# Moving the expert search of tiles 0 and 1 in a decoder layer: a part per step in tile 3's attention, and tile 1's scores through the side banks

## What is computed

```
xn = rms_norm(h); proj = xn @ w_in                       # q, k, v of both mixers, indexer, gates
y_a = diff_attention(...) @ w_branch_a                   # 4 heads, two softmaxes each
y_b = dsa_attention(... top 128 keys by the indexer) @ w_branch_b   # 8 heads
h = h + (sigmoid(gate_a) * y_a + sigmoid(gate_b) * y_b) @ w_out
hn = rms_norm(h)
q = hn @ w_query                                         # 8 heads x 2 halves of 64
s = q . sub_keys                                         # 8 x 2 x 128 scores per token
s1, i1 = top_k(s[..., 0, :], 16); s2, i2 = top_k(s[..., 1, :], 16)
expert = 16 best of the pairs s1 + s2                    # per head, of 128 * 128 experts
g = softmax(best sums)
h = h + sum over picks of g * gelu(u[expert] . hn) * v[expert]
```

## Time and profile before

| | |
|---|---|
| median of 3 runs | 1787.48 us (1783.99 to 1790.81) |
| the profiled execution: its time, its span | 1786.4 us, 1784.5 us |
| TensorE (PE) busy | 1718.6 us, 96% of the span |
| VectorE (DVE) busy | 1333.6 us, 75% |
| ScalarE (ACT) busy | 702.6 us, 39% |
| POOL busy | 697.6 us, 39% |
| chain that ended last | PE 64%, DVE 16% of the span |

### The profile page before, as it was taken

How to read it: one execution, slowest core, us unless ns; L and a number is a source line. 1 busy time by engine, 2 the same in 40 slices (tenths; PEclk the granted TensorE clock), 3 DMA queues, 4 the chain that set the end, 5 groups by cost and what they waited for, 6 DMA issues and landing times.

```text
span 1784.5 us, 27405 instructions
## 1 busy us (share of the span) xinstructions
PE 1718.6 (96%) x10077; PEld 1538.3 (86%) x10077; DVE 1333.6 (75%) x3000; ACT 702.6 (39%) x1042; POOL 697.6 (39%) x478
## 2 busy tenths in 40 slices
PE   8999998989898999999999999999999999999998
PEld 6778776555655779999999999999999999999998
DVE  5475945647557779899999805974888888888886
ACT  5334235232323234366346535553333333333332
POOL 5244330000001235687777766786522222222220
PEclk9999998989998999999999999999999999999999
DMA  4122213525443645699989998998998889888882
GB/s 162 45 93 95 75 44 119 188 95 180 149 146 139 208 143 161 188 349 326 353 283 318 307 358 310 358 335 300 387 347 335 323 330 336 322 332 334 321 333 111
DMA packets 154183, 429.88 MB, mean 241 GB/s; under 512 B 15312, under 2 KB 49744, under 8 KB 149728
## 3 DMA queue, kind: packets, MB, share of 16 engines
q1 hardware_dynamic: 117040, 294.23, 47.3%
q0 software_dynamic: 36864, 134.23, 19.9%
q10 hardware_dynamic: 176, 0.07, 0.0%
HBM read 384.44 MB, written 44.04 MB: 240 GB/s over the span
## 4 chain that ended last, share of the span: by engine, by line
PE 64%; DVE 16%; ACT 2%; issue 2%; DMA 1%; DVEq 0%; ACTq 0%
PE psum L2055 30%; PE psum L1210 6%; PE psum L1280 6%; PE psum L1282 5%; PE psum L1281 5%; PE psum L1197 3%; PE psum L1309 2%; PE psum L1110 2%; DVE rows_sb L1726 2%; DVE hits L1759 2%; DVE hot L1840 2%; DVE hits L1756 2%; DVE pick L1760 1%; DVE hot L1837 1%; PE psum L1166 1%
## 5 line engine op out<-in xcount | busy, mean ns | idle before, releaser
L1538 POOL TENSOR_TENSOR ul<-u,uh 128x1024 fp32r<-128x1024 f32 x128 | 320.4, 2506 | 457.3 <-ACT uh L1448 455.8
L1280 PE MATMUL psum<-split,uh 128*128 128x384 f32 x1024 | 353.9, 346 | 1.1 <-POOL ul L1538 1.1
L2055 PE MATMUL psum<-wh,vl 128*128 128x384 f32 x1024 | 343.6, 336 | 0.0
L1282 PE MATMUL psum<-split,ul 128*128 128x384 f32 x1024 | 343.3, 335 | 0.0
L1281 PE MATMUL psum<-split,uh 128*128 128x384 f32 x1024 | 342.9, 335 | 0.0
L2028 POOL DMA_INDIRECT v_row<-in_v,tri x128 | 146.1, 1141 | 357.8 <-DVE mixed L2127 349.9
L1280 PEld LDWEIGHTS psum<-split,uh 128*128 128x128 f32 x1024 | 192.8, 188 | 3.1 <-issue 1.4
L1281 PEld LDWEIGHTS psum<-split,uh 128*128 128x128 f32 x1024 | 193.0, 188 | 1.4 <-issue 1.4
L1282 PEld LDWEIGHTS psum<-split,ul 128*128 128x128 f32 x1024 | 192.6, 188 | 0.0
L2055 PEld LDWEIGHTS psum<-wh,vl 128*128 128x128 f32 x1024 | 192.3, 188 | 0.0
L2055 PE MATMUL psum<-wl,vh_first 128*128 128x384 f32 x512 | 173.2, 338 | 0.0
(11 more groups left out here) (315 smaller groups left out, 3232.0 us busy)
## 6 DMA issues: line engine op xcount, KB each, us to landing
u<-in_u SPq DMA_DIRECT2D x128, 512.0 KB
v<-in_v SPq DMA_DIRECT2D x64, 1024.0 KB
act_mat<-act_w SPq DMA_DIRECT2D x128, 192.0 KB
w<-act_mat SPq DMA_DIRECT2D x64, 384.0 KB
wraw<-in_w_wide SPq DMA_DIRECT2D x18, 1024.0 KB, 5.0
gate<-gate_mat SPq DMA_DIRECT2D x128, 128.0 KB
w_low<-in_w_branch_b SPq DMA_DIRECT2D x8, 1024.0 KB, 5.1
w_high<-in_w_branch_a SPq DMA_DIRECT2D x8, 1024.0 KB, 5.3
```

The costliest lines, as they stand in the source:

```text
L1280: nc.tensor.matmul(out, high[:, c], dense_x[0][:, c], start=(c == 0), stop=False)
L1282: last = nc.tensor.matmul(out, low[:, c], dense_x[0][:, c], start=False, stop=(c == DC - 1))
L1538: nc.gpsimd.tensor_tensor(ul[:, n % U_COLS], u[:, n % U_COLS], uh[:, n % UH_COLS].bitcast(F32), ALU.subtract).then_inc(s["u_low"], 1)
L2055: mm = nc.tensor.matmul(bank(m, c)[:, 0:WIDTH], lhs, rhs, start=first and k == 0 and p == 0, stop=final and p == 2)
```

## The change

Tile 0's search parts get other steps: finding at 36 to 40 instead of 36, 37, 40, 41, 43; pairing and the first two parts of the best at 41; picking out at 43, 44, 45, 46 instead of 49, 49, 50, 51; settling at 47 instead of 52. Tile 1's scores are no longer multiplied in one go at step 50 but in two products on the side banks at steps 45 and 46, as tile 0's are at 33 and 34, and ScalarE copies them one step later each; its search begins at step 48 instead of 52 and is settled at 58 instead of 63. TensorE's step 47 now waits for those copies before it uses the side banks. The picks of tile 0 are turned one pair of columns sooner (`AHEAD[1]` 14 instead of 15), and with them every later start, turn and the gathers.

```diff
-SCORE_FIRST, SCORE_FIRST_REST, SCORE_SECOND = 33, 34, NT * UNITS + 2
-FIND_AT = ((36, 37, 40, 41, 43), (52, 53, 54, 55, 56))
-PAIR_AT = (44, 57)
-BEST_AT = ((44, 47, 48, 48, 48), (58, 58, 59, 59, 60))
-PICK_AT = ((49, 49, 50, 51), (61, 61, 62, 62))
-SETTLE_AT = (52, 63)
+SCORE_FIRST, SCORE_SECOND = (33, 45), (34, 46)
+FIND_AT = ((36, 37, 38, 39, 40), (48, 49, 50, 51, 52))
+PAIR_AT = (41, 53)
+BEST_AT = ((41, 41, 42, 42, 43), (53, 54, 54, 54, 55))
+PICK_AT = ((43, 44, 45, 46), (55, 55, 56, 57))
+SETTLE_AT = (47, 58)
...
-AHEAD = (0, 15, 9, 9)
+AHEAD = (0, 14, 9, 9)
...
                     elif j == TURN_HN:
-                        if t == 1:
-                            pe.wait_ge(s["s_out"], 2)
+                        if 1 <= t <= 2:
+                            pe.wait_ge(s["s_out"], 2 * t)
...
-                if step == SCORE_FIRST:
-                    pe.wait_ge(s["keys_loaded"], 16)
-                    pe.wait_ge(s["streamed"], 4)
-                    route(0, 0, SIDE)
-                if step == SCORE_FIRST_REST:
-                    pe.wait_ge(s["s_out"], 1)
-                    route(0, 1, SIDE)
-                if step == SCORE_SECOND:
-                    pe.wait_ge(s["scores_used"], len(PLAN))
-                    pe.wait_ge(s["pT_ready"], len(ALL_UNITS))
-                    route_halves(1, 0, 2)
+                for r in range(2):
+                    if step == SCORE_FIRST[r]:
+                        pe.wait_ge(s["keys_loaded"], 16)
+                        pe.wait_ge(s["streamed"], 2 * (r + 2))
+                        route(r, 0, SIDE)
+                    if step == SCORE_SECOND[r]:
+                        pe.wait_ge(s["s_out"], 2 * r + 1)
+                        route(r, 1, SIDE)
                 if step >= FIRST_COLUMN:
                     column(step - FIRST_COLUMN)
-            pe.wait_ge(s["s_out"], 4)
+            pe.wait_ge(s["scores_used"], len(PLAN))
             route_halves(2, 2, SIDE)
...
-                if step == SCORE_FIRST + 1:
-                    score_out(0, 0, SIDE)
-                if step == SCORE_FIRST_REST + 1:
-                    score_out(0, 1, SIDE)
+                for r in range(2):
+                    if step == SCORE_FIRST[r] + 1:
+                        score_out(r, 0, SIDE)
+                    if step == SCORE_SECOND[r] + 1:
+                        score_out(r, 1, SIDE)
...
-                if step == BEST_AT[0][-1] + 1:
-                    exps(0)
+                for r in range(2):
+                    if step == BEST_AT[r][-1] + 1:
+                        exps(r)
...
-                if step == SCORE_SECOND + 1:
-                    score_out(1, 0, 0)
-                    score_out(1, 1, 2)
                 if step > FIRST_COLUMN:
                     column(step - 1 - FIRST_COLUMN)
-                if step == BEST_AT[1][-1] + 1:
-                    exps(1)
```

More of the change, by code:

```diff
@@ L876 @@
 FIRST_PAIR = TAIL_COLUMNS // 2
-assert TAIL_COLUMNS % 2 == 0 and FIRST_PAIR + 7 < TURNS_AT[1]
+assert TAIL_COLUMNS % 2 == 0 and FIRST_PAIR + 6 < TURNS_AT[1]
 assert TAIL_AT < PAIRS and AHEAD[2] > STORES and AHEAD[3] > STORES
```

## The result

The changed kernel takes 1801.11 us in the median of four runs (1799.08 to 1803.69), the kernel before 1785.93 us beside it (1783.99 to 1790.81): ratio 1.0077, with a 95% interval of 1.0051 to 1.0103. That is 15.2 us slower, where +4.5 was forecast, and above the end of the range. The profiled execution took 1799.37 us, span 1797.6 us.

The account below looks back on a forecast made before the run. TensorE was taken to bound the kernel, over 90% busy in nearly all slices. The terms 6.4 - 2.1 + 0.2 gave +4.5 us, 1790.9 on the profiled execution and 1792.0 for the median; range 1785 to 1798.

Parts of the forecast that it names:

- The late chain of steps 44 to 48: VectorE's added picking out and settling make TensorE wait for the normed and scaled rows, 6.4 us in all; chance 0.62.
- the clock term: Query product behind the two pauses in steps 47 and 48: low clock costs 0 to 1.2 us more, taken as 0.
- the prediction's list of signs: What the profile should show, including waits of 3 us and more for step 47's row and about the same before the query product.
- the sentence on the clock: The skill's "activity releases the throttle": by it alone the query product would run wholly at the low level, some 6 us more.
- The old product, -2.1: Step 50: tile 1's old scores product goes away, saving 2.06 us, with 3.45 us as the other end.
- Steps 51 to 62: Between attention and last search: tile 1's search called done long before; its new place got no cost.
- The first turn, +0.2: Turn of tile 0's picks, two columns sooner: slack of 6.9 us becomes 0.1 us late, taken as 0.2; gathers cost 0.
- The second turn: Next turn of picks among the columns, called tile 2's: it keeps its distance, so its wait of 1.82 us stays.
- Filled gaps: Rival: tile 1's products on the side banks keep the clock full around steps 45 to 48, -5.5 us, 1782.0; chance 0.09.
- Late picks: Rival: POOL's conversions hold the last search's VectorE passes, tile 0's picks 4.3 us late, +10.0 us, 1797.5; chance 0.15.
- Hidden: Rival: VectorE's new parts fit between the products and the clock stays, about 0, 1787; chance 0.14.

Follow-up runs that it names:

- e3: The changed kernel with tile 0's last part of picking out at step 48 instead of 46 and its settling at 49 instead of 47: 1794.18 us, ratio 1.0043.
- f1: The kernel before with only tile 1's scores through the side banks at steps 45 and 46, search and AHEAD as before: 1786.15 us, ratio 1.0005.
- e1: The changed kernel with tile 1 settled at step 60 instead of 58, behind tile 3's normed row: 1795.68 us, ratio 1.0048.
- h3: The kernel before with AHEAD[1] 14 instead of 15 and nothing else: 1789.24 us, ratio 1.0019.
- h2: The kernel of f3 run once more for a second profile: 1790.23 us in one run.
- e2: The changed kernel with AHEAD[1] back at 15: 1801.44 us, ratio 1.0076.
- f3: The kernel of e4 with AHEAD[1] 14 again instead of 15: 1790.83 us, ratio 1.0034.
- e4: The changed kernel with tile 0's last picking out at step 48, settling at 49 and 60, and AHEAD[1] 15: 1784.91 us, ratio 0.9995.
- p1: The kernel before, unchanged, run again for a second profile: 1789.73 us in one run.
- f2: The kernel before with only tile 0's search at the new early steps, tile 1 and AHEAD as before: 1795.17 us, ratio 1.0049.

## Why the prediction was wrong, step by step

**The late chain of steps 44 to 48: right.** The normed row was forecast at 552.65 us and came at 549.04; in this execution step 42 was 2.9 us earlier, so 0.7 us of a difference is left. From step 42 on, the transposes came 36.55 us later where it had been 32.55, +4.0 against +4.6; the query product +5.2 against +6.4; the transposes of tile 2's queries +5.8, with the product's 9.10 us against 8.26, which is the clock term of 0 to 1.2, taken as 0, at +0.8. Both waits stood where they were to stand; they were 3.52 and 1.34 us instead of both about 3. For the second the prediction's list of signs didn't follow from its own sum, which left 6.4 - 4.6 = 1.8 us for it. Its estimate from the sentence on the clock, some 6 us more for the product, did not come: 9.10 us is 0.84 more. e3 shows the cause: with the last part of picking and the settling out of the chain both waits for VectorE are gone, and 1.56 us for ScalarE are left.

**The old product, -2.1: mis-sized, about -0.8.** From the transposes of tile 2's queries to the first column it was 5.45 us before and 4.70 after, -0.75. The product had covered ScalarE's copy of the queries, and without it TensorE waits 1.10 us for that copy (581.00), and it does so at the low clock. f1 shows the same 1.10. The stage comes to +5.1 where the terms gave +4.3.

**Steps 51 to 62: the step that failed.** The prediction followed tile 0's search only. It said of tile 1's that it "is now done long before", took that as slack for the last search, and had no term for its new place. But the picking out and the settling of tile 1 now stand in steps 55 to 58, in front of tile 3's root and row of step 59, where they had stood in steps 61 to 63, behind them. It is the same mechanism as the one it had priced for tile 0, one tile on, and it cost 7.9 us with the clock behind it (e1: 7.6 of it gone by one number). Without this stage the measured median would lie at 1793.2, within 1.2 us of the forecast. The window that was read for this stretch, busy 280.29 of 283 us, said that TensorE had no slack there, so a new wait costs its full length; it was read as "the sum of its matmuls, which the change only reorders".

**The first turn, +0.2: too small.** The stage took +2.4 us, with AHEAD 14 alone 3.5 (h3), 2.1 in h2, and with AHEAD 15 0.0 (e2). The doubled picks were ready in time, about as forecast (754.9 us for a turn at 755.63). What was costed at "0, at most some tenths" was the rest of the turn, the gathers: they could not all "move with the turn", since the row numbers of tile 3 were no longer ready ahead of them, and the rows landed late for VectorE's dot products (h3). Before, these numbers were ready at 743.3 us for a gather at 749.90, a slack of 6.6 us, as small as the 6.9 us that the sum worked out for the doubled picks, and the turn moved by 8.4.

**The second turn, "its wait of 1.82 us [...] stays": not borne out.** The prediction names it tile 2's; it is the turn of tile 1's picks (pair 32, now 31), which VectorE doubles only behind the whole search of tile 2 (`chosen(3, 2)` stands ahead of `double_picks(2)`), so its wait is for that search. It was 3.69 here. It was 3.3 in a second profile of the kernel before, absent in h3 and in f3, and 4.7 in h2, which is f3 once more, so it moves from execution to execution by up to 5 us, and one profile gives no value for it.

**The rivals.** *Filled gaps* is not borne out as a rule. In e4 and f3, with tile 1's pair of products there and the chain not late, TensorE kept the full clock from 487 to 572 us and the stage was 2.4 us shorter than before; but in h2, the same program up to there, it did not, and the stage was 0.2 us shorter. The row it rested on, the full clock with tile 0's pair, did not come again in p1 (0.81 for the same work). With the old search beside it (f1) the granted clock was 0.78 from 546 to 556 us and nothing was gained. *Late picks* gave the nearer number, 1797.5, for the wrong reason: some passes were held longer (2.892 us on average had become 3.385), but the whole search took 66.0 us where it had been 66.7, and the picks weren't late. *Hidden* is out, by the waits of 3.52 and 1.34 us for VectorE.

**What stays open.** Why AHEAD 14 costs nothing in the changed kernel (e2) and 5.9 us on top of e4 (f3). The first gates are slower with AHEAD 14 in both; the rest may lie in how often the later turns wait, which the medians of many executions hold and one profile doesn't show. Why the second turn waits in one execution and not in the next is open too, and so is what sets the clock at steps 45 to 48. Tile 1's search moved alone wasn't tried: its list of finds shares memory with tile 0's picks, so it can't begin before those are done.

## What to carry to other kernels

When one queue of work is moved forward, walk every item of it past everything that it now stands ahead of, not only the first; the second tile's small instructions cost about as much here as the first tile's large ones. A stretch in which the bounding engine is 99% busy is where a moved wait costs its full length, and here the low clock behind it half as much again. When a turn is moved forward, check each thing that was ready ahead of it, not only one: here the gathers' row numbers had as little slack as the doubled picks, and what TensorE showed as a wait for VectorE was a DMA's landing passed on. Before a forecast rests on a wait of one profile, take a second profile of the same kernel and see which waits are in both.

## What the runs showed of the chip that was not expected

- The granted clock isn't given by TensorE's own recent work alone. From 515.56 to 540.6 us TensorE's rows are the same to 0.01 us in the first profile of before and in f2; the level fell at 545.7 in one and at 540.3 in the other, where it stayed low for 24 us. In e4 and h2 the wait at step 47 is 1.56 us in both; one kept the full clock, the other was low for 6.8 us.
- The granted clock of the same program in the same place differs between executions (0.81 and 0.97 from 358 to 393 us in the two profiles of before, worth 3.7 us there; 1.1 us of it are left at step 42).
- A VectorE instruction of 128x1 elements took 2.11 us instead of 0.16, and a cast of 128x128 2.45 instead of 0.23, beside a conversion of POOL's of 2.4 us. So in a chain of small instructions it is the chance of meeting such a conversion that sets the time.
